# Gathering the rows of an expert block whole instead of in quarters

## The reference, cut to what matters

```python
x_rows = x_pad[row_tok].reshape(n_blocks, MOE_BLOCK, d)   # rows gathered by token number

def expert_block(args):
    e, xb = args
    hu = xb @ w_up[e] + b_up[e]                            # 1024 -> 2048
    g = jnp.minimum(hu[:, :D_FF], SWIGLU_LIMIT)
    lin = jnp.clip(hu[:, D_FF:], -SWIGLU_LIMIT, SWIGLU_LIMIT)
    glu = g * jax.nn.sigmoid(SWIGLU_ALPHA * g)
    return ((lin + 1.0) * glu) @ w_down[e] + b_down[e]     # 1024 -> 1024

y = jax.ops.segment_sum(y_rows * row_gate[:, None], row_tok, num_segments=t + 1)[:t]
```

## Time and profile before

| what | value |
|---|---|
| median of 3 runs | 3347.1 us |
| lowest, highest | 3343.88, 3348.02 us |
| span of the profiled execution | 3352.8 us |
| PE matmul busy | 2825.7 us (84%) |
| DVE busy | 1291.4 us (39%) |
| ACT busy | 898.9 us (27%) |
| POOL busy | 280.1 us (8%) |
| DMA | 581.92 MB, mean 174 GB/s |
| experts' stage, by the first and last gather | 583 to about 1743 us |

### The profile page before, as it was taken

One profiled execution on the slowest core, in us unless ns is written; L12 is line 12 of the kernel. 1 busy time (PEld: TensorE's weight loads), 2 busy tenths in 40 slices (PEclk: granted clock), 3 DMA queues, 4 the chain that ended last, 5 costly groups with the idle time before them and its releaser, 6 DMA issues. The chain is left out here.

```text
span 3352.8 us, 65854 instructions
## 1 busy us (share of the span) xinstructions
PE 2825.7 (84%) x25476; PEld 2041.8 (61%) x25477; DVE 1291.4 (39%) x2922; ACT 898.9 (27%) x1856; POOL 280.1 (8%) x365
## 2 busy tenths in 40 slices
PE   6987675888888867989969597899999688899998
PEld 4965475444444423545538475778887566778886
DVE  1236554223222212333323474444443365643343
ACT  2233321112121101222213143343332133532232
POOL 1000000122221211222210100000000100000000
PEclk7996676899999967999989698999999788899999
DMA  6243006899999999799972300022221210022221
GB/s 181 77 154 117 1 13 252 318 385 344 382 386 387 344 391 388 241 353 386 361 260 84 96 1 26 26 76 101 101 101 60 69 51 1 26 73 85 95 101 50
DMA packets 299974, 581.92 MB, mean 174 GB/s; under 512 B 35780, under 2 KB 74372, under 8 KB 299764
## 3 DMA queue, kind: packets, MB, share of 16 engines
q1 hardware_dynamic: 279876, 557.27, 45.5%
q0 software_dynamic: 15792, 21.34, 2.9%
q10 hardware_dynamic: 4098, 0.49, 0.1%
HBM read 562.25 MB, written 16.78 MB: 173 GB/s over the span
## 5 line engine op out<-in xcount | busy, mean ns | idle before, releaser
L1909 PE MATMUL moe_up<-expert_w,mod 128*32 128x256 f32 x3856 | 243.1, 397 | 24.1 <-DMA expert_w<-in_exp_w_up 18.2
L1909 PE MATMUL moe_up<-ring,mod 128*32 128x256 f32 x3184 | 200.7, 402 | 30.9 <-issue 19.2
L1972 ACT ACTIVATE mod<-mod 128x128 f32<-128x128 f32 x158 | 48.9, 310 | 637.8 <-DVE mod L2004 637.8
L360 PE MATMUL mlp_bank<-hT_hi,mlp_w 128*128 128x512 f32 x512 | 199.4, 390 | 0.0
L362 PE MATMUL mlp_bank<-hT_hi,mlp_w 128*128 128x512 f32 x512 | 199.2, 389 | 0.0
L361 PE MATMUL mlp_bank<-hT_lo,mlp_w 128*128 128x512 f32 x512 | 199.2, 389 | 0.0
L360 PE MATMUL mlp_bank<-mlp_w,mlp_u_hi 128*128 128x512 f32 x512 | 199.2, 389 | 0.0
L361 PE MATMUL mlp_bank<-mlp_w,mlp_u_hi 128*128 128x512 f32 x512 | 199.2, 389 | 0.0
L362 PE MATMUL mlp_bank<-mlp_w,mlp_u_lo 128*128 128x512 f32 x512 | 199.2, 389 | 0.0
L1909 PEld LDWEIGHTS moe_up<-expert_w,mod 128*32 128x32 f32 x3856 | 122.7, 113 | 120.7 <-issue 27.1
L2002 DVE TENSOR_TENSOR mod<-moe_up,mod 128x256 f32<-128x256 f32 x158 | 67.1, 425 | 320.8 <-PE moe_up L1909 317.6
(11 more groups left out here) (522 smaller groups left out, 5765.1 us busy)
## 6 DMA issues: line engine op xcount, KB each, us to landing
expert_w<-in_exp_w_up SPq DMA_DIRECT2D x194, 512.0 KB
ring<-in_exp_w_up SPq DMA_DIRECT2D x150, 512.0 KB
ring<-in_w_ff SPq DMA_DIRECT2D x32, 2048.0 KB, 8.7
expert_w<-in_exp_w_down SPq DMA_DIRECT2D x47, 1024.0 KB, 11.1
ring<-in_exp_w_down SPq DMA_DIRECT2D x39, 1024.0 KB, 10.8
moe_w<-in_exp_w_up SPq DMA_DIRECT2D x74, 512.0 KB
ring<-in_ada_w SPq DMA_DIRECT2D x12, 2048.0 KB, 11.9
hT<-in_exp_w_up SPq DMA_DIRECT2D x48, 512.0 KB
```

The lines of the kernel that those rows point to most:

```text
L360: nc.tensor.matmul(out, lhsT.hi, rhs.hi, start=(i == 0), stop=False)
L1909: mm = nc.tensor.matmul(up[half][quarter[q], 0:2 * UNITS], rowsT[:, f % 2, quarter[f // 2]], chunk[r][c][:, :, j, q * UNITS:(q + 1) * UNIT ...
L1972: nc.scalar.activation(sig[:, half], pre[:, half, 0:UNITS], ACT.Sigmoid, scale=ALPHA).then_inc(sig_ready, 1)
```

## The change

The indirect DMA gathers whole rows: 32 of 4 KB, on 32 partitions. `rows` becomes 32 x 1024 and moves to the last row of `k.mod`, on partitions 0 to 31; the list holds token numbers, so the instruction that made quarter-row numbers of them goes. The turning becomes eight transposes, one for each 128 columns of the rows: the stationary operand is 32 partitions x 128 columns, the moving one the 32x32 corner of the identity. They fill the same 256 columns of the PSUM bank, as 8 groups of 32 (`turn_r[:, f * BR:(f + 1) * BR]`), and ACT's copy, still 128 x 256, goes to `rowsT[:, f, :]`, from which the matmuls take the same numbers as before. Since `rows` now lies where the output scale lay, POOL waits for `scale_laid` before the first gather. PE signals a new semaphore (`rows_seen`) between the wait for the gather and the transposes of a loop's block. The scatter, the weights and all matmuls stay.

```diff
@@ route_stages, DVE
             chain(nc.vector.tensor_tensor(spare[:], spare[:], number[:], ALU.add))
-            chain(nc.vector.tensor_scalar(number[:], number[:], float(PARTS), k.part_no[:], ALU.mult, ALU.add))
             chain(nc.vector.tensor_copy(k.row_token[:], number[:]))
@@ expert_stage
-        rows, y = work[:, 0, :], work[:, 1, :]
-        rowsT, hidT, sig, hid = (work[:, n, :].rearrange("p (h n) -> p h n", n=P) for n in range(2, 6))
+        rows, y = k.mod[0:BR, 3, :], work[:, 1, :]
+        hidT, sig, hid = (work[:, n, :].rearrange("p (h n) -> p h n", n=P) for n in range(3, 6))
+        rowsT = work[:, 2, :].rearrange("p (f n) -> p f n", n=BR)
...
-        index, place = sb("index", [P, 1], U32), sb("place", [P, 1], U32)
+        index, place = sb("index", [BR, 1], U32), sb("place", [P, 1], U32)
...
-        h2_parts = h2_dram.rearrange("s (q n) -> (s q) n", q=PARTS)
@@ gather, POOL
-                nc.gpsimd.tensor_copy(index[:], k.row_token[:, bass.ds(b, 1)]).then_inc(indexed, 1)
+                nc.gpsimd.tensor_copy(index[:], k.row_token[0:BR, bass.ds(b, 1)]).then_inc(indexed, 1)
                 pool.wait_ge(indexed, copies)
                 pool.sem_inc(waited, 1)
-                pool.indirect_dma_start(rows, None, h2_parts,
+                pool.indirect_dma_start(rows, None, h2_dram,
                                         bass.IndirectOffsetOnAxis(ap=index[:], axis=0)).then_inc(gathered, 16)
...
+            pool.wait_ge(scale_laid, PARTS)
             gather(0, 1)
@@ turn_rows, PE
-                for j in range(2):
-                    tr = nc.tensor.transpose(turn_r[:, j * P:(j + 1) * P], rows[:, j * P:(j + 1) * P], k.ident[:])
+                for f in range(ND):
+                    tr = nc.tensor.transpose(turn_r[:, f * BR:(f + 1) * BR], rows[:, f * P:(f + 1) * P], k.ident[0:BR, 0:BR])
                 tr.then_inc(rows_turned, 1)
@@ up_chunk, PE
-                        mm = nc.tensor.matmul(up[half][quarter[q], 0:2 * UNITS], rowsT[:, f % 2, quarter[f // 2]],
+                        mm = nc.tensor.matmul(up[half][quarter[q], 0:2 * UNITS], rowsT[:, f, :],
@@ run, PE
                     pe.wait_ge(gathered, b * 16 + 32)
+                    pe.sem_inc(rows_seen, 1)
                     turn_rows()
@@ take_rows, ACT
-                nc.scalar.activation(rowsT, turn_r[:, 0:2 * P].rearrange("p (j r) -> p j r", r=P), ACT.Copy).then_inc(rows_taken, 1)
+                nc.scalar.activation(rowsT, turn_r[:, 0:ND * BR].rearrange("p (f r) -> p f r", r=BR), ACT.Copy).then_inc(rows_taken, 1)
```

More of the change, by code:

```diff
@@ L1803, in expert_stage @@
         gathered, y_stored = k.gathered, k.y_stored
-        rows_turned, rows_taken = sem("rows_turned"), sem("rows_taken")
+        rows_turned, rows_taken, rows_seen = sem("rows_turned"), sem("rows_taken"), sem("rows_seen")
         chunk_done, gate_ready, sig_ready, hid_ready, up_taken = sem("chunk_done"), sem("gate"), sem("sig"), sem("hid"), sem("up_taken")
```

## The result

The changed kernel takes **3399.1 us** (median of 4 runs, 3390.2 to 3405.5), the kernel before 3346.2 us beside it: 1.57% slower, ratio 1.0157 with a 95% interval from 1.0138 to 1.0176. Forecast were 3356 us, with a range up to 3373. The direction was right, the size was not: +53 us in place of +9. The profiled execution has a span of 3401.8 us (3352.8 before), 49.0 us more.

What follows compares the result with a forecast made beforehand. The bound was taken as the latency loop through the gather in blocks with weights streaming. 10.8 - 4 + 0 + 2.1 = +8.9 us, put on the median 3347.1, gave 3356 us, range 3339 to 3373.

Steps and rivals of the forecast that it cites:

- The bound: Experts' stage, blocks with weights streaming: latency loop through the gather binds, about 0.8 us above PE's own work.
- The count of blocks: Blocks that count: 12 of 47 in the first stretch (590 to 1340 us), 28 of 32 in the second; together 40.
- SP's 13 waits: SP's waits for PE to free a weight chunk in the first stretch; one block taken for each, say 12.
- +10.8: Us for transposes and signal in the gather loop: 40 blocks x 0.27 us.
- Transposes and signal: On PE, between landing and down chunk 10: transposes 0.22 us more, signal 0.05, together +0.27 us a block.
- POOL's issue: POOL's issue of the gather, 1.00 us: -0.2 us in every second block, -0.1 x 40 = -4 us.
- The transfer moves the same 128 KB ... I take 0: Gather's landing: its excess is waiting behind weights, which neither row size changes; 0 us.
- rival C: Gather's destination narrower: 32 partitions served at half rate, +0.34 us in the loop, +13.6 us, 3370; 18%.
- The start: Stage's first gather waits until DVE has laid the scale aside: +2.1 us, bounds 0 and 2.5.
- Rivals A: POOL's issue shrinks with the indices, all 0.44 us go: -4.7 us, 3342; 20% together with D.
- B: Gather's landing shorter by over 0.5 us, fewer pieces per engine: likelier -10 us, 3337; 10%.
- D: Eight transposes and signal fit into PE's waiting time, only the start is left: 3349; within A's 20%.

Runs made afterwards that it cites:

- z2: Kernel before with POOL copying 128x480 numbers between the index copy and the gather's issue, lengthening the loop; 3372.2 us, ratio 1.0072.
- y1: Kernel before with the gather issued ahead of the scatter on POOL, two gathers before the loop; 3323.7 us, ratio 0.9932.
- x2: Kernel before with the change's turning alone: rows_seen signal and eight 32x128 transposes, gather as before (wrong rows turned); 3368.0 us, ratio 1.0064.
- x4: Kernel before with PE's rows_seen signal alone, between the wait for the gather and its two transposes; 3350.5 us, ratio 1.0012.
- x1: Kernel before with the change's gather alone: 32 whole rows to partitions 0 to 31, late start, turning as before (wrong rows); 3382.3 us, ratio 1.0098.
- x3: As x1, but the 32 rows land on partitions 0, 4, ... 124; 3351.5 us, ratio 1.0004 to the kernel before.
- y4: x1 with the gather issued ahead of the scatter as in y1; 3344.1 us, ratio 0.9994 to the kernel before.
- z3: x3 with the gather issued ahead of the scatter as in y1; 3327.0 us, ratio 0.9933 to the kernel before.
- z1: As x1, but the 32 rows land on partitions 0, 2, ... 62; 3380.5 us, ratio 1.0100 to the kernel before.
- y2: The changed kernel with the gather issued ahead of the scatter as in y1; 3354.1 us, ratio 1.0022 to the kernel before.
- y3: The changed kernel with rows on partitions 0, 4, ... 124, turned by eight matmuls against every fourth identity column; 3460.6 us, ratio 1.0334.

## Why the prediction was wrong

**The bound was right.** The loop through the gather sets the streaming blocks: lengthening it by another engine's 0.43 us cost 24.5 us (z2), taking the landing out of it brought the period to PE's own 11.74 us (y1).

**The count of blocks was wrong.** The prediction took 40, by discounting the first stretch to SP's 13 waits. The measure was in the earlier trace rows already: PE waited 62 times, the stage's first wait (7.5 us) among them, so 61 times in the loop. x2 (19.1 us at 0.30 us a block: 64) and z2 (57; 0.42 us in each of the 61) show that all of them count. A stretch whose mean DMA share is 1.01 still holds blocks that the weights do not bound. What was lost in the 61 was not given back in the 17 others in x2 (346.2 and 346.4 us); in z2's trace 8.1 of 25.6 us were, and in after's 3.7 of 52.0. The 61 blocks alone turn +10.8 into +16.5.

**Transposes and signal**, 0.27 us a block: right. Measured 0.22 + 0.10, and 0.29 in x2's periods. The fp32 run of the earlier trace rows priced the loads well: from the first transpose's load to the down chunk's 0.59 us were forecast, and 0.61 measured (x2, mean; 0.58 from the transpose itself, which starts 0.03 us behind its load). By an estimate from the rule of the Trainium skill (TensorE: Matmul & The Clock Gate, LDWEIGHTS) the six further loads alone would have taken 0.64 us; the trace disagrees, all eight took 0.57 us. The signal alone was 1.6 us (x4).

**POOL's issue**: -0.10 us in every block. The forecast was -0.2 in every second one, so its mean came out by luck. Its working was thin: it compares the gather with two plain DMAs of 0.61 and 0.56 us (and speaks of three), while others issued beside those took up to 1.10 us.

**The step that failed is "The transfer moves the same 128 KB ... I take 0".** The same bytes in the same 32 packets cost 31 us more when they went to partitions 0 to 31 (x1 less x3). I had read the excess of the landing as waiting behind weights, which the destination could not touch. It can. This is rival C, which I gave 18% and 3370 us. Its size per gather, 0.34 us, was near: landing +0.36 us between x3 and x1. It was too cheap for two reasons: 40 blocks in place of 61, and the remark that it is worse "if the engines hold up weights meanwhile" had no price, where y4 against z3 shows 19 us by that way alone. The two are not to be added: y4's order leaves more blocks to the weights than x1's. In x1 itself, against x3, the 61 waiting blocks took 25.1 us more (0.41 each, 0.36 of it landing) and the other 17 took 6.6 more.

**The half clock was not in the sum.** 12 blocks in place of 6 add some 19.6 - 8.0 = 11.6 us of down chunks (all 79 blocks, above 1.55 us each), part of x1's and x2's sums and of what they make together. Neither a longer wait alone (z2: 6) nor the turning alone (x2: 7) brought it; x3 and x4 had 5 each, x1 9, z1 10, the whole change 12 and 13. The counts of x1 to z2 are of one trace each. Why a particular block falls to 1.2 GHz stays open.

**The start**: right, +2.0 us against +2.1. (The expectations of x1 and y2 reckon with 1.3, which is what the span's own clock shows and not the stage's.) Rivals A, B and D are out: the issue shrank by 0.10 and not 0.44 us, the landing grew, and no turning fitted into the wait. Of what the profile was to show, the turning (0.6), landing to transpose (0.1), issue (0.8 to 1.0) and some 60 waits came out; the landing median of 6.1 was on C's threshold, the mean 6.23 over it, and the first stretch changed by more than 4 us (357 in place of 370 GB/s over 750 us is some 26 us of transfers), which the prediction had named as its refutation. Gathers in the second stretch came every 13.5 us (median), not every 12.7.

The forecast with what the runs gave: x1's 33.4 (31 for the place, 2.6 for the rest, x3) and x2's 19.1 us, on 3346 = 3399 us.

## What to carry to other kernels

Look where a small transfer lands, not only how many bytes and pieces it has: 32 rows of 4 KB to partitions 0 to 31, or to every second one up to 62, cost 31 us here that the same rows over the whole range of partitions did not, by their latency and by what they took from the transfers beside them. When a closed loop of latencies bounds a stage, count the blocks in which the engine waits, from the profile, and let none off for the stretch's average. And before making the links of such a loop shorter, look whether one can be taken out: issuing the gather ahead of the scatter gained 23 us, with one more column in the lists and the semaphore counts to match.

## What the runs showed of the hardware beyond that

- The form of the gather did not matter: 128 quarter rows or 32 whole rows went as 32 packets of 4096 bytes. What 32 indices saved was 0.10 us of issue (0.99 to 0.89 us). A destination with gaps took back 0.03 us (x3 0.92, z1 0.93).
- An fp32 matmul of 128x128 by 32 columns ran as two instructions, 16 of them in 1.9 us (y3); a transpose of as many columns ran as one, eight of them in 0.6 us (after).
- A signal on TensorE between a wait and the transposes behind it held the first load back by 0.06 us (landing to load 0.04 us before, 0.10 in x4), 1.6 us in all.
